# A decoder layer on one core: the first modulation shared out anew between TensorE and VectorE, an S5 exponential on GpSimd, other chunk and load orders

## The chip, the cores and the metric

One core of a Trainium2 chip runs the whole program. The metric is the device time of one execution in microseconds (us); what the kernel before is judged by is the median of three executions.

## What is computed

One layer (DEPTH is 1) of a hybrid decoder trunk in float32 over 512 tokens of width 1024, batch 1. The parts that matter here:

```python
def _split_in(z): ...        # z = h @ w_in + b_in, cut into u, qk, v, o, i, f, q, k, v, f, gates
dt = jnp.exp(log_dt.astype(f32))[:, None]        # first S5 exponential
mag = jnp.exp(dt * are)                          # second S5 exponential
ang = dt * aim
abar_r, abar_i = mag * jnp.cos(ang), mag * jnp.sin(ang)
# _rmsnorm: x * rsqrt(mean(x * x) + EPS) * g
# the layer (adaLN): mod = silu(c) @ mod_w + mod_b, six parts of 1024 columns:
#   h = rmsnorm(x) * norm1_g * (1 + scale) + shift        <- the first two parts
#   x = x + gate * mixer(h);  the second half of the layer, SwiGLU, uses the other parts
```

The mixer sends h through one projection `w_in` (5134 columns), runs three token mixers on it (S5 state space, mLSTM, forgetting attention), merges them by gates and projects by `w_out`; a SwiGLU FFN of width 2816 follows. The first modulation, its 2048 columns `shift` and `scale`, stands ahead of everything: without it there is no h and no projection.

## The kernel before, in words

The program is written engine by engine; each engine runs its list in order and waits on semaphores. Activations lie transposed: `h` is 8 blocks (`KB`) of 128 channels by 512 tokens. Each float32 factor is split in a high and a low part, and a product of 128 by 128 weights with a block of h is three matmuls of 512 columns (lines 1623 to 1625: h_lo by whi, h_hi by whi, h_hi by wlo).

**Chunks.** `w_in` is used in 42 chunks of up to 128 columns, in the order of `A_CHUNKS`: first chunk f (the 14 gate columns, spread over a full tile that GpSimd zeroed before), then u (2), mqk (3), mv (3) and so on. For a chunk s, SP loads `raw`, ScalarE makes the high part (`hi(s)`, line 636), VectorE the low part (`lo(s)`, line 1128), TensorE multiplies (24 matmuls), ScalarE moves the sum out (`evac(s)`). Chunks 0 and 1 are multiplied side by side, block by block of h, because h only then comes into being; from chunk 2 on one follows the other. ScalarE's list around a chunk t is: hi(t), evac(t-3). Chunk s needs lo(s) and evac(s-2). SP's load of chunk s (4 or later) waits until chunk s-4 is multiplied.

**The opening.** SP loads four tiles of x (`xtok`, 0.5 MB each), then eight slabs of `mod_w` (`modA`, `modB`, 1 MB each, 128 rows by 2048 columns) with the small loads of `rows1` behind slab 2 and the three loads of chunk f (line 449, 1024 pieces of 16 or 24 bytes each) behind slab 5. ScalarE's queue loads `rows2` (c, a_re, a_im, log_dt, d). TensorE turns `rows2`, VectorE copies it (`s5c`), ScalarE makes silu(c) (`cf`), squares the tiles of x and takes the root. VectorE meanwhile: exponential of log_dt, 1/root, scaling of the four tiles of x (line 1018, for which TensorE's transposes wait), `vectors()`, the second exponential, the S5 angle scalars (lines 983 to 1040), and then the shift half of the modulation, slab by slab (columns 0 to 1023, lines 987 and 1118). TensorE takes the scale half by `mod_rows(k)`: per slab two matmuls of one weight column and 512 columns (line 1642). The two halves become columns by 8 matmuls each (lines 1667 and 1675) into one bank; VectorE adds the bias (line 1135) and forms the gain (line 1137); only then do ScalarE (lines 734, 735) and VectorE (lines 1147, 1150) make h_hi and h_lo, block by block.

**Behind it** VectorE's list goes lo(2), lo(3), `coefficients()` (S5), four of the eight angle tables, two of the four blocks of B, lo(4), two blocks of B, lo(5), four tables, lo(6) and on.

`keep_clock(n)` is a helper that gives TensorE n matmuls of 256 columns whose result nobody reads; before, it is used at the start of the FFN only.

Of the kernel before, what the change touches and what calls it, by code (L numbers as in the profile page):

```python
# [23 lines left out]
P = 128  # L24
# [31 lines left out]
A_CHUNKS = ([("f", 0)] + [("u", i) for i in range(2)] + [("mqk", i) for i in range(3)]  # L56
# [10 lines left out]

S_UP = NA
# [16 lines left out]
def build(nc, x, c, mod_w, mod_b, norm1_g, norm2_g, w_in, b_in, a_re, a_im, log_dt, b_re, b_im,  # L85
# [3 lines left out]
    with es:  # L89
# [175 lines left out]
        dve_step = sem("dve_step")  # L265
        t_rows = sem("rows_transposed")
# [168 lines left out]
        def _(sp_):  # L437
            for t in range(NT):
                sp_.dma_start(xtok[:, t], x[t * P:(t + 1) * P, :]).then_inc(s_x[t], 16)
            for k in range(KB):  # L440
                sp_.dma_start((modA, modB)[k // 4][:, k % 4], mod_w[k * P:(k + 1) * P, 0:2 * D]
                              ).then_inc(s_mod0[k], 16)
                if k == 2:
                    for src, n, r in ROWS1[5:]:
                        sp_.dma_start(rows1[r:r + n, :], src).then_inc(s_rows1, 16)
                if k == 5:
                    sp_.wait_ge(s_pad, 1)
                    for c0, n, at0 in ((OFF_MF, MH, 0), (OFF_FF, FH, MH), (OFF_MI, MH, 32)):
# [85 lines left out]
        def _(pool):  # L534
            nc.gpsimd.memset(ident[:], 0.0).then_inc(s_const, 1)
# [13 lines left out]
            nc.gpsimd.memset(sst[:, :, :, 0:1], 0.0).then_inc(s_const, 1)  # L549

# [38 lines left out]
        def _(act):  # L589
# [9 lines left out]
            act.dma_start(rows2[96:104, :], row_view(c[0], 8)).then_inc(s_rows, 16)  # L599
# [337 lines left out]
        def _(dve):  # L937
# [1181 lines left out]
```

## Time and profile before

| | us |
|---|---|
| executions | 882.35, 880.01, 877.83 |
| median | 880.01 |
| the profiled execution, its own time | 878.05 |
| its span in the profile | 876.3 |
| TensorE busy | 848.2 (97%) |
| VectorE busy | 440.8 (50%) |
| ScalarE busy | 324.2 (37%) |
| GpSimd busy | 32.9 (4%) |

The span is what the engines' records cover; 1.75 us of the execution lie around it. The median lies 1.96 us above the profiled execution. A timeline row gives start, duration (both us), engine, line and operation, what is written and read with its shape, how often, and in brackets the idle time ahead and what ended it.

### The profile page before, as it was taken

To read this page: it belongs to the slowest core of one execution; us is meant where nothing else is said; L and a number is where in the kernel's file an instruction comes from. 1 tells how busy PE (TensorE), PEld (TensorE's weight loads), DVE (VectorE), ACT (ScalarE), POOL (GpSimd) and SP (SyncE) were. 2 spreads that over 40 slices of the span, in tenths; PEclk is the share of its full clock that TensorE was granted. 3 is DMA by queue.
4 is the path that set the end of the run, shared out by engine and by line. 5 is a ranking of instruction groups with operands and counts; after the bars stand their busy time and mean duration, and the time that the engine had idled before them with its cause. 6 is when DMAs were issued, how large, how long until landed. Compare 5 with 4: busy or idle time off the path is not lost.

```text
span 876.3 us, 10481 instructions
## 1 busy us (share of the span) xinstructions
PE 848.2 (97%) x3914; PEld 678.3 (77%) x3914; DVE 440.8 (50%) x719; ACT 324.2 (37%) x477; POOL 32.9 (4%) x46
## 2 busy tenths in 40 slices
PE   4899999999999999999999999999999999999996
PEld 1477888877878677777888878888888888888886
DVE  4889977246768653334883354333333333322222
ACT  3555444443222543433333544333333332222221
POOL 1010000000000000000001110000000000000110
PEclk9899999999999999999999999999999999999999
DMA  9823422257785112114323324333333333333322
GB/s 366 231 76 88 105 73 73 73 158 253 261 288 169 48 49 65 57 45 148 97 73 121 96 56 114 96 96 96 96 96 96 96 96 90 92 107 90 98 76 96
DMA packets 149372, 100.67 MB, mean 115 GB/s; under 512 B 11072, under 2 KB 142552, under 8 KB 148312
## 3 DMA queue, kind: packets, MB, share of 16 engines
q1 hardware_dynamic: 149096, 100.14, 37.9%
q8 instruction: 22, 0.36, 0.2%
q14 instruction: 14, 0.11, 0.0%
q10 hardware_dynamic: 240, 0.06, 0.0%
HBM read 97.03 MB, written 2.10 MB: 113 GB/s over the span
## 4 chain that ended last, share of the span: by engine, by line
PE 88%; DVE 6%; ACT 3%; issue 1%; DMA 1%; ACTq 0%; DVEq 0%
PE bank L1623 25%; PE bank L1625 25%; PE bank L1624 25%; PE bank L1832 2%; PE bank L1762 1%; PE bank L1854 1%; PE bank L1782 1%; PE bank L1793 1%; PE bank L1642 1%; DVE wlo L1128 1%; PE bank L1879 1%; PE bank L1845 1%; PE bank L1830 1%; DMA rows<-in_s_d 1%; ACT whi L636 1%
## 5 line engine op out<-in xcount | busy, mean ns | idle before, releaser
L1623 PE MATMUL bank<-h_lo,whi 128*128 128x512 f32 x712 | 286.7, 403 | 4.0 <-DVE h_lo L1150 2.2
L1625 PE MATMUL bank<-h_hi,wlo 128*128 128x512 f32 x712 | 279.3, 392 | 0.0
L1624 PE MATMUL bank<-h_hi,whi 128*128 128x512 f32 x712 | 278.8, 392 | 0.0
L1623 PEld LDWEIGHTS bank<-h_lo,whi 128*128 128x128 f32 x712 | 134.9, 189 | 34.8 <-issue 5.9
L1624 PEld LDWEIGHTS bank<-h_hi,whi 128*128 128x128 f32 x712 | 135.0, 190 | 28.8 <-issue 1.7
L1625 PEld LDWEIGHTS bank<-h_hi,wlo 128*128 128x128 f32 x712 | 134.5, 189 | 29.0
L1128 DVE TENSOR_TENSOR wlo<-raw,whi 128x1024 fp32r<-128x1024 f32 x61 | 74.4, 1223 | 104.3 <-ACT whi L636 104.3
L636 ACT ACTIVATE whi<-raw 128x1024 fp32r<-128x1024 f32 x61 | 64.2, 1055 | 153.2 <-PE bank L1625 110.1
L1625 PE MATMUL bank<-a_hi,wlo 128*128 128x512 f32 x176 | 68.5, 389 | 0.0
L1623 PE MATMUL bank<-a_lo,whi 128*128 128x512 f32 x176 | 68.5, 389 | 0.0
L1624 PE MATMUL bank<-a_hi,whi 128*128 128x512 f32 x176 | 68.5, 389 | 0.0
L1585 DVE TENSOR_TENSOR wlo<-raw,whi 128x1024 fp32r<-128x1024 f32 (+1 forms) x24 | 27.3, 1137 | 76.3 <-ACT whi L904 76.3
L1566 DVE TENSOR_TENSOR aa<-sil,bank 128x512 f32<-128x512 f32 x22 | 15.1, 687 | 99.0 <-PE bank L1625 99.0
L1578 DVE TENSOR_TENSOR wlo<-raw,whi 128x1024 fp32r<-128x1024 f32 x40 | 49.0, 1225 | 28.3 <-ACT whi L897 27.0
L897 ACT ACTIVATE whi<-raw 128x1024 fp32r<-128x1024 f32 x40 | 42.1, 1053 | 30.2 <-DMA raw<-in_ffn_w 30.2
L904 ACT ACTIVATE whi<-raw 128x1024 fp32r<-128x1024 f32 (+1 forms) x24 | 23.7, 988 | 67.9 <-DMA raw<-in_ffn_w 67.9
L888 ACT ACTIVATE a_hi<-aa 128x512 f32 x20 | 12.6, 632 | 96.8 <-DVE aa L1566 96.8
L1384 DVE SCALAR_TENSOR_TENSOR macc<-slab,cf,macc 128x1024 f32<-128x1024 f32 x28 | 36.0, 1287 | 6.5 <-DMA slab<-in_mod_w 4.6
L709 ACT ACTIVATE pf<-bank,nmx 128x128 f32<-128x128 f32 (+3 forms) x24 | 12.6, 527 | 69.6 <-PE bank L1845 48.9
L1624 PEld LDWEIGHTS bank<-a_hi,whi 128*128 128x128 f32 x176 | 33.0, 188 | 6.9
L1625 PEld LDWEIGHTS bank<-a_hi,wlo 128*128 128x128 f32 x176 | 33.0, 188 | 6.9
L1623 PEld LDWEIGHTS bank<-a_lo,whi 128*128 128x128 f32 x176 | 33.0, 188 | 6.8
(325 smaller groups left out, 983.5 us busy)
## 6 DMA issues: line engine op xcount, KB each, us to landing
raw<-in_ffn_w SPq DMA_DIRECT2D x60, 512.0 KB, 3.8
raw<-in_w_in SPq DMA_DIRECT2D x44, 512.0 KB, 4.0
slab<-in_mod_w SPq DMA_DIRECT2D x32, 512.0 KB, 6.0
modA<-in_mod_w SPq DMA_DIRECT2D x4, 1024.0 KB, 12.1
modB<-in_mod_w SPq DMA_DIRECT2D x4, 1024.0 KB, 11.1
raw<-in_w_out SPq DMA_DIRECT2D x8, 512.0 KB, 3.7
raw<-in_ffn_w SPq DMA_DIRECT2D x8, 384.0 KB, 3.3
xtok<-in_x SPq DMA_DIRECT2D x4, 512.0 KB, 5.2
```

Of the source, the lines that this page charges most:

```text
L636: A(w_high(s), raw[:, s % 4], ACT.Copy).then_inc(w_hi, 1)
L897: A(whi4[:, s % 4], raw[:, s % 4], ACT.Copy).then_inc(w_hi, 1)
L904: A(whi4[:, s % 4, 0:nk], raw[:, s % 4, 0:nk], ACT.Copy).then_inc(w_hi, 1)
L1128: V.tensor_tensor(wlo[:, s % 4], raw[:, s % 4], w_high(s).bitcast(F32), ALU.subtract).then_inc(w_lo, 1)
L1384: ins = V.scalar_tensor_tensor(out=macc[g][:], in0=slab[:, q % 4], scalar=cf[:, k:k + 1], in1=macc[g][:], op0=ALU.mult, op1=ALU.add)
L1566: V.tensor_tensor(aa[:, u], sil[:, u], ps[2 * u + 1][:], ALU.mult).then_inc(s_act, 1)
L1578: V.tensor_tensor(wlo[:, s % 4], raw[:, s % 4], whi4[:, s % 4].bitcast(F32), ALU.subtract).then_inc(w_lo, 1)
L1585: V.tensor_tensor(wlo[:, s % 4, 0:nk], raw[:, s % 4, 0:nk], whi4[:, s % 4, 0:nk].bitcast(F32), ALU.subtract).then_inc(w_lo, 1)
L1623: mm(dst, w_h, m_l, start=first, stop=False)
L1624: mm(dst, w_h, m_h, start=False, stop=False)
L1625: return mm(dst, w_l, m_h, start=False, stop=last)
L1832: mm(b, qpad[:, h, t * P:(t + 1) * P], kf[:, h // 2, 0:ln], start=False, stop=True).then_inc(s_fs, 1)
```

## The change

Six things:

- **Chunk order.** f stands behind the three mqk chunks, as chunk 5 (`S_F`). Its three loads are issued in the loop, once chunk 1 is multiplied, and not between the slabs. hi and lo of it handle 14 columns in two instructions each, not 128. The fill of its tile on GpSimd is gone.
- **Loads.** c and a_re go through SP, between the first and the second tile of x (ScalarE's queue keeps a_im, log_dt, d). The loads of `rows1` come behind slab 1. The loads of chunks 0, 1, 2 come right behind slab 7. The 16 moves of u come at s = 8, not 9.
- **Second exponential on GpSimd**, `decay()`: 30 instructions of 128x8 in a chain (VectorE has fused forms, GpSimd takes two instructions for those), from T3 = dt * a_re, which VectorE now makes as soon as dt is there. `coefficients()` waits for its end (`s_mag`).
- **First modulation.** VectorE sums columns 0 to 1279 into `macc1st`, TensorE 1280 to 2047 (512 and 256 wide). On VectorE the angle scalars and slab 0 come ahead of the scaling of x, slabs 1 to 7 behind it, `vectors()` behind slab 2; slab 7 is taken in three pieces.
- **h in two halves.** The columns for blocks 0 to 3 (shift and scale) go to bank 7, those for 4 to 7 to bank 6; bias and gain are formed half by half (`mod_halves`). ScalarE and VectorE begin blocks 0 to 3 with the first half; lo(1) stands between the low parts of blocks 0 and 1.
- **Fill matmuls.** `keep_clock(7)` ahead of the slabs, `keep_clock(2, 3)` ahead of chunk 0.

VectorE's list from the end of the first exponential to lo(1). Before (`sp` are the S5 scalars, `modA` and `modB` the slabs, `gs_55` the gain):

```order
L990 SCALAR_TENSOR_TENSOR sp<-sp,spi 128x8 [waits dve_step]
L1016 RECIPROCAL rstd<-rstd 128x4 [waits std_ready,dve_step]
L1018 TENSOR_SCALAR xtok<-xtok,rstd 128x1024 [waits dve_step]
L1018 TENSOR_SCALAR xtok<-xtok,rstd 128x1024 x3
L965 COPY vec<-bank 128x128 [waits rows_transposed]
L983 TENSOR_TENSOR sp<-sp,s5c 128x8
L1040 TENSOR_SCALAR sp<-sp 128x8 [waits dve_step]
L987 TENSOR_SCALAR modA<-modA,cf 128x1024 [waits mod_first_loaded0,silu_c_ready,dve_step]
L1118 SCALAR_TENSOR_TENSOR modA<-modA,cf 128x1024 [waits mod_first_loaded1,dve_step]
L1128 TENSOR_TENSOR wlo<-raw,whi 128x1024 [waits w_hi_ready] x2
L1135 TENSOR_TENSOR modc<-bank,vec 128x16 [waits mod_first_columns]
```

and now:

```order
L1071 TENSOR_TENSOR sp<-sp,s5c 128x8
L1088 TENSOR_SCALAR sp<-sp 128x8 [waits dve_step]
L1172 TENSOR_SCALAR macc1st<-modA,cf 128x1280 [waits mod_first_loaded0,silu_c_ready,s5_scalar_inputs]
L1163 RECIPROCAL rstd<-rstd 128x4 [waits std_ready,dve_step]
L1165 TENSOR_SCALAR xtok<-xtok,rstd 128x1024 x3
L1174 SCALAR_TENSOR_TENSOR macc1st<-modA,cf,macc1st 128x1280 [waits mod_first_loaded1]
L1174 SCALAR_TENSOR_TENSOR macc1st<-modB,cf,macc1st 128x512 [waits mod_first_loaded7,dve_step]
L1174 SCALAR_TENSOR_TENSOR macc1st<-modB,cf,macc1st 128x256
L1190 TENSOR_TENSOR wlo<-raw,whi 128x1024 [waits w_hi_ready]
L1198 TENSOR_TENSOR modc<-bank,vec 128x2x4 [waits mod_first_columns]
L1223 TENSOR_TENSOR h_lo<-hs,h_hi 128x512 [waits h_hi_ready,dve_step]
L1190 TENSOR_TENSOR wlo<-raw,whi 128x1024 [waits w_hi_ready]
```

The angle scalars and slab 0 moved ahead of the scaling of x, the second exponential left, and only lo(0) now stands ahead of the first bias and gain.

SP's queue from the slabs to the loop over chunks. Before:

```order
L441 DMA modA<-in_mod_w 128x2048 x3
L445 DMA rows_136<-in_b_in 24x128
L441 DMA modB<-in_mod_w 128x2048 x2
L449 DMA raw<-in_w_in 128x8x4 [waits padding_zeroed]
L449 DMA raw<-in_w_in 128x8x6
L449 DMA raw<-in_w_in 128x8x4
L441 DMA modB<-in_mod_w 128x2048 x2
L451 DMA raw<-in_w_in 128x8x128
L452 DMA bsrc<-in_s_b_re 128x8x16
```

and now:

```order
L453 DMA modA<-in_mod_w 128x2048 x2
L457 DMA rows_138<-in_b_in 24x128
L453 DMA modB<-in_mod_w 128x2048 x4
L459 DMA raw<-in_w_in 128x8x128 x3
L460 DMA bsrc<-in_s_b_re 128x8x16
L484 DMA raw<-in_w_in 128x8x128 [waits w_chunk_multiplied]
L480 DMA raw<-in_w_in 128x8x4 [waits w_chunk_multiplied]
L480 DMA raw<-in_w_in 128x8x6
L480 DMA raw<-in_w_in 128x8x4
L484 DMA raw<-in_w_in 128x8x128 [waits w_chunk_multiplied] x3
```

The piecewise loads of f left the place ahead of slabs 6 and 7 and stand between the loads of chunks 4 and 6.

TensorE's list between the last slab and chunk 0. Before, and below it now:

```order
L1667 MATMUL bank<-ones,modrow 128x1 [waits mod_row_copied]
L1667 MATMUL bank<-ones,modrow 128x1 x3
L1675 MATMUL bank<-ones,modA 128x1 [waits mod_first_summed_dve]
L1675 MATMUL bank<-ones,modA 128x1 x7
L1623 MATMUL bank<-h_lo,whi 128x512 [waits h_lo_ready,w_lo_ready]
```

```order
L1737 MATMUL bank<-ones,macc1st 128x1 [waits mod_first_summed_dve,columns_copied]
L1737 MATMUL bank<-ones,macc1st 128x1 x3
L1737 MATMUL bank<-ones,macc1st 128x1 [waits mod_first_summed_dve]
L1743 MATMUL bank<-ones,modrow 128x1 [waits mod_row_copied]
L1743 MATMUL bank<-ones,modrow 128x1 x3
L1731 MATMUL bank<-ones,ident 128x256 x2
L1696 MATMUL bank<-h_lo,whi 128x512 [waits w_lo_ready,h_lo_ready]
```

The sixteen column matmuls stay sixteen, in two groups of eight, and two fill matmuls follow.

The diff, cut:

```diff
-A_CHUNKS = ([("f", 0)] + [("u", i) for i in range(2)] + [("mqk", i) for i in range(3)]
+A_CHUNKS = ([("u", i) for i in range(2)] + [("mqk", i) for i in range(3)] + [("f", 0)]
...
+        DVE_COLS = 1280
+        PE_COLS = ((1280, 1792), (1792, 2048))
...
-            for t in range(NT):
+            sp_.dma_start(xtok[:, 0], x[0:P, :]).then_inc(s_x[0], 16)
+            sp_.wait_ge(s_zero, 1)
+            sp_.dma_start(rows2[96:104, :], row_view(c[0], 8)).then_inc(s_rows, 16)
+            sp_.dma_start(rows2[0:8, :], a_re.rearrange("(i g) n -> i (g n)", g=2)).then_inc(s_rows, 16)
+            for t in range(1, NT):
...
-                if k == 5:
-                    sp_.wait_ge(s_pad, 1)
-                    for c0, n, at0 in ((OFF_MF, MH, 0), (OFF_FF, FH, MH), (OFF_MI, MH, 32)):
-                        sp_.dma_start(raw[:, 0, :, at0:at0 + n],
...
+                if s == S_F:
+                    for c0, n, at0 in ((OFF_MF, MH, 0), (OFF_FF, FH, MH), (OFF_MI, MH, 32)):
+                        sp_.dma_start(raw[:, s % 4, :, at0:at0 + n],
...
-                if s == 9:
+                if s == 8:
                     sp_.wait_ge(s_evac, A_CHUNKS.index(("u", 1)) + 1)
...
+            pool.wait_ge(s_t3, 1)
+            decay()
...
-                A(w_high(s), raw[:, s % 4], ACT.Copy).then_inc(w_hi, 1)
+                if s == S_F:
+                    A(w_high(s)[:, :, 0:10], raw[:, s % 4, :, 0:10], ACT.Copy)
+                    A(w_high(s)[:, :, 32:36], raw[:, s % 4, :, 32:36], ACT.Copy).then_inc(w_hi, 1)
...
-            act.wait_ge(s_modc, 2)
             for k in range(KB):
+                act.wait_ge(s_modc, 2 + 2 * (k // 4))
...
             def coefficients():
 
                 dve.wait_ge(s_trig, 2)
+                dve.wait_ge(s_mag, 1)
...
+            for k in range(KB):
+                if k == 1:
+                    dve.wait_ge(s_std, 1)
+                    link(V.reciprocal(rstd[:], rstd[:]))
...
+                if k == 3:
+                    vectors()
                 dve.wait_ge(s_mod0[k], 16)
...
             lo(0)
-            lo(1)
...
+            mod_halves(0)
             dve.wait_ge(s_xnc, KB)
             for k in range(KB):
+                if k == 1:
+                    lo(1)
+                if k == 2:
+                    mod_halves(1)
...
+            keep_clock(7)
             for k in range(KB):
                 mod_rows(k)
...
+            mod_row_columns(7, 0, range(10, 12)).then_inc(s_mod1, 1)
+            mod_row_columns(6, 0, range(12, 14))
+            pe.wait_ge(s_modd, 3)
+            mod_columns(6, range(4, 8))
+            pe.wait_ge(s_mrowc, 2)
+            mod_row_columns(6, 1, range(14, 16)).then_inc(s_mod1, 1)
+            keep_clock(2, 3)
```

## Rows read from the trace of the kernel before

**Rows 1.** The page, part 2: granted TensorE clock in 40 slices of 21.9 us

```profile
PEclk9899999999999999999999999999999999999999
```

**Rows 2.** Timeline of TensorE: opening, chunks 0 to 4, fill matmuls of the FFN

```profile
12.24 5.82 PE L1642 MATMUL bank<-modA,cf 128*1 128x512 f32 x8 [2.94 <-DMA modA<-in_mod_w]
...
18.75 1.09 PE L1653 MATMUL bank<-ident,xtok 128*128 128x128 f32 x8 [0.43 <-DVE xtok L1018]
19.78 1.88 PE L1642 MATMUL bank<-modA,cf 128*1 128x512 f32 x4
...
34.75 1.94 PE L1667 MATMUL bank<-ones,modrow 1*128 1x1 f32 x16
36.62 3.04 PE L1675 MATMUL bank<-ones,modA 128*128 128x1 f32 x16
41.86 0.77 PE L1623 MATMUL bank<-h_lo,whi 128*128 128x512 f32 x1 [2.20 <-DVE h_lo L1150]
...
55.85 0.47 PE L1623 MATMUL bank<-h_lo,whi 128*128 128x512 f32 x1 [0.19 <-ACT fz L645]
...
67.98 0.50 PE L1623 MATMUL bank<-h_lo,whi 128*128 128x512 f32 x1 [0.96 <-DVE wlo L1128]
...
502.11 1.89 PE L1659 MATMUL bank<-ones,ident 128*128 128x256 f32 x8
```

**Rows 3.** Timeline of VectorE, from the scaling of x to lo(4)

```profile
15.74 0.18 DVE L1016 RECIPROCAL rstd<-rstd 128x4 f32<-128x4 f32 x1 [2.67 <-ACT rstd L618]
15.96 2.74 DVE L1018 TENSOR_SCALAR xtok<-xtok,rstd 128x1024 f32<-128x1024 f32 x4
18.61 0.28 DVE L965 COPY vec<-bank 128x128 f32<-128x128 f32 x1
...
23.28 0.17 DVE L983 TENSOR_TENSOR sp<-sp,s5c 128x8 f32<-128x8 f32 x1
...
26.53 0.75 DVE L987 TENSOR_SCALAR modA<-modA,cf 128x1024 f32<-128x1024 f32 x1
27.32 3.92 DVE L1118 SCALAR_TENSOR_TENSOR modA<-modA,cf 128x1024 f32<-128x1024 f32 x3
...
39.70 0.17 DVE L1135 TENSOR_TENSOR modc<-bank,vec 128x16 f32<-128x16 f32 x1 [0.90 <-PE bank L1675]
...
49.49 0.69 DVE L1150 TENSOR_TENSOR h_lo<-hs,h_hi 128x512 fp32r<-128x512 f32 x1 [0.47 <-ACT h_hi L735]
...
66.71 1.22 DVE L1128 TENSOR_TENSOR wlo<-raw,whi 128x1024 fp32r<-128x1024 f32 x1
```

**Rows 4.** Timeline of ScalarE

```profile
34.86 0.59 ACT L718 ACTIVATE modrow<-bank 1x512 f32<-1x512 f32 x1 [0.27 <-PE bank L1642]
35.35 1.99 ACT L636 ACTIVATE whi<-raw 128x1024 fp32r<-128x1024 f32 x2
40.11 0.81 ACT L735 ACTIVATE h_hi<-xnT,modc,gs 128x512 fp32r<-128x512 f32 x1 [2.77 <-DVE gs L1137]
```

**Rows 5.** Timeline of the DMA queues: when each issue began, how long it held its queue

```profile
2.75 0.41 ACTq L603 DMA_DIRECT2D rows<-in_s_d  x1
...
7.94 16.39 SPq L449 DMA_DIRECT2D raw<-in_w_in  x3
...
25.95 2.90 SPq L452 DMA_DIRECT2D bsrc<-in_s_b_re  x1
```

**Rows 6.** Line 449 (the three loads of f) and line 441 (the slabs): time from issue to landing

```profile
DMA to landing us min/median/max: 6.4/16.5/17.2
...
DMA to landing us min/median/max: 5.2/12.1/17.3
```

**Rows 7.** Windows of 1 us: length, each engine's busy time, granted clock, DMA share, GB/s

```profile
37.00:38.00 1.00, 1.00 (x8) 1.00 (x8) 1.00 (x2) 0.34 (x1) 0.00 (x0) 0.62 0.64 128
47.00:48.00 1.00, 1.00 (x5) 0.75 (x5) 0.86 (x2) 0.87 (x3) 0.00 (x0) 0.76 0.00 0
```

**Rows 8.** GpSimd groups by shape: busy and mean ns of one | idle before

```profile
L585 POOL TENSOR_TENSOR sqa<-sqa,sq 128x512 f32<-128x512 f32 x5 | 6.4, 1285 | 63.3 <-ACT sq L910 63.3
```

More of the change, by code:

```diff
@@ L401, in build @@
         for s in range(S_F1):
-            count[s % 4] += 16 * (3 if s == 0 or S_UP <= s < S_OUT else 1)
+            count[s % 4] += 16 * (3 if s == S_F or S_UP <= s < S_OUT else 1)
             SLOT_LOADS[s] = count[s % 4]
@@ L598, in _ @@
             act.wait_ge(s_zero, 1)
-            act.dma_start(rows2[96:104, :], row_view(c[0], 8)).then_inc(s_rows, 16)
-            act.dma_start(rows2[0:8, :], a_re.rearrange("(i g) n -> i (g n)", g=2)).then_inc(s_rows, 16)
             act.dma_start(rows2[32:40, :], a_im.rearrange("(i g) n -> i (g n)", g=2)).then_inc(s_rows, 16)
@@ L1008, in exact_exp @@
                 stt(o, c_(POL), 1.0, two_k, ALU.add, ALU.mult)
-                if om1 is not None:
-                    tt(om1, c_(POL), two_k, ALU.mult)
-                    stt(om1, two_k, -1.0, om1, ALU.add, ALU.add)
-            exact_exp(c_(DT), None, ldt)
-            dve.wait_ge(s_std, 1)
-            link(V.reciprocal(rstd[:], rstd[:]))
-            for t in range(NT):
-                V.tensor_scalar(xtok[:, t], xtok[:, t], rstd[:, t:t + 1], None, ALU.mult).then_inc(s_xn, 1)
-            vectors()
-            tt(c_(T3), c_(DT), are, ALU.mult)
-            exact_exp(c_(MAG), c_(EM1), c_(T3))
+            exact_exp(c_(DT), ldt)
+            V.tensor_tensor(c_(T3), c_(DT), are, ALU.mult).then_inc(s_t3, 1)
             tt(c_(ANG), c_(DT), aim, ALU.mult)
@@ new lines, in mod_halves @@
+            def mod_halves(half):
+                k0 = 4 * half
+                dve.wait_ge(s_mod1, half + 1)
+                pair = modc[:, 0:16].rearrange("p (v k) -> p v k", k=KB)[:, :, k0:k0 + 4]
+                V.tensor_tensor(pair, ps[7 - half][:, 0:16].rearrange("p (v k) -> p v k", k=KB)[:, :, k0:k0 + 4],
+                                vec[:, V_MOD:V_MOD + 16].rearrange("p (v k) -> p v k", k=KB)[:, :, k0:k0 + 4],
+                                ALU.add).then_inc(s_modc, 1)
+                dve.wait_ge(s_modc, 2 * half + 1)
+                V.scalar_tensor_tensor(out=gs1[:, k0:k0 + 4], in0=modc[:, 8 + k0:12 + k0], scalar=1.0,
+                                       in1=vec[:, V_N1 + k0:V_N1 + k0 + 4], op0=ALU.add, op1=ALU.mult
+                                       ).then_inc(s_modc, 1)
+                dve.wait_ge(s_modc, 2 * half + 2)
@@ L1640, in mod_rows @@
                 pe.wait_ge(s_mod0[k], 16)
[L1641 to L1643 removed]
+                for n, (c0, c1) in enumerate(PE_COLS):
+                    ins = mm(ps[4 + n][0:1, 0:c1 - c0], cf[:, k:k + 1], (modA, modB)[k // 4][:, k % 4, c0:c1],
                              start=(k == 0), stop=(k == KB - 1))
```

155 lines of the change are left out of this document (100 added, 55 removed).

## The prediction

> **What bounds the kernel now.** First the busy shares and the clock row of the page: TensorE is busy 97% of the span at full clock except near the start [rows 1]. Then TensorE's timeline, for its gaps: of its 28 us of idle time the long gaps lie before 68 us, and the 808 us behind it are the same work after the change. So the change is worth what it takes from one moment, the start of chunk 4 at 67.98 [rows 2]. Everything else is read backwards from there.
>
> At 67.98 TensorE had waited 0.96 us for VectorE's lo(4), which ended at 67.93; the last h_lo ended at 50.18 [rows 3]. VectorE works those 17.75 us without a break, on lo(2), lo(3) and S5, none of which the change shortens. TensorE needs for its own part: chunk 0 from 41.86, chunks 2 and 3 from 55.85, 11.2 us, ready at 67.0. So two chains end together there, VectorE's last, TensorE's 1 us ahead. Both start with h_hi of block 0 at 40.11 [rows 4], and that with the last columns of the modulation.
>
> Before it: the SP queue is held 16.39 us by the three loads of f, and slabs 6 and 7 are issued only at 24.4 [rows 5]. Slab 0 landed at 12.2, slab 5, issued at about 7.4 with the longest way, 17.3, at 24.7: 2.5 us per slab [rows 6]. They were not what was late: VectorE came to slab 0 only at 26.53, behind scaling, second exponential and angle scalars, and had all at 36.5.
>
> **The change part by part.** All on the clock of the profiled execution (span 876.3, its own time 878.05).
>
> *rows2.* ScalarE's queue issues d at 2.75; two issues ahead of it (0.6 and 0.3 us) go to SP. Gain between 0 (if only the shared engines count) and 0.9 us; I take 0.65, since the way from issue to landing, 5.7 us, is far longer than an issue and needn't shrink. VectorE ended its first exponential at 13.07 (15.74 less 2.67), now 12.4.
>
> *VectorE up to slab 7.* Angle scalars 23.28 to 26.1 [rows 3], with T3 2.9 us: 15.3. Slab 0 on 1280 columns 0.95 (0.75 for 1024): 16.3. Reciprocal 0.2, scaling 2.74: x is scaled at 19.25, against 18.7 before, 0.55 later. Slabs 1 to 6: 3.92 / 3 = 1.31 for 1024 columns, 1.62 for 1280, so 6 times 1.62 = 9.7, with vectors() 0.6: 29.6. Slab 7 lands at 24.7 + 2 * 2.5 = 29.7, the same moment; its three pieces (0.7, 0.3, 0.6) are done at 30.4, 30.7 and 31.3. Before: 36.5. Most of this is order and the exponential (3.85 us from 19.2 to 23.1), not the split, which costs VectorE 7 * 0.31 + 0.2 = 2.4 us.
>
> *TensorE.* From 18.75 to 34.75 it did four pairs of transposes (1.03 us each), six slabs and 1.1 us of waiting [rows 2], so 1.8 us per slab; with 768 columns of 1024, 1.36. The 1.1 us went with ScalarE, which stood in its list at the sines behind the angle scalars; these come early now. From 19.4: 4.1 + 8.2, rows done at 31.7. Eight columns of the first group take 2.3 us (half of 1.94 + 3.04, less for the full clock): 34.1.
>
> *ScalarE and lo(0).* Two row copies (0.59 and, on 256 columns, 0.35 [rows 4]) end at 32.3; hi(0) 1.0: 33.35; lo(0) 1.22: 34.6. It stands ahead of the bias, so it decides, not the columns at 34.1. Bias and gain 0.4 (39.70 to 40.11): h_hi(0) starts at 35.05, against 40.11: 5.05 us earlier. Half of h stands first, but this half costs lo(1) and a second bias between blocks: hs(3) on ScalarE waits for h_lo(1), 0.4 us later than before. Last h_lo at 35.05 + 10.07 + 0.4 = 45.6, against 50.18. VectorE's chain then gives lo(4) at 45.6 + 17.75 = 63.35.
>
> *TensorE's chain.* The second group of eight columns at half clock ends at 36.6. The fill of two: eight records are 1.89 at full clock [rows 2], so 4 are 0.95, or 1.8 at half: start of chunk 0 at 38.3. Before, the clock fell to half at 37.4 and came back at 47.4 [rows 7], 2.6 us into the sixteen column matmuls. The same sixteen stand there now, so I let it fall at 34.4 and return at 44.4. Then 14 matmuls at 0.427 and 34 at 0.228: chunk 1 done at 52.1. With 11.2 for chunks 2 and 3 and 0.3 for the evacuation: 63.6. Chunk 4 starts at the later of the two chains, 63.65: **4.3 us earlier.** If the clock doesn't fall, TensorE is ready at 59 and VectorE's 63.35 decides: 4.6.
>
> *The f loads.* Issued when chunk 1 is done, 52.2. Their landing is needed by hi(5), ahead of evac(2) in ScalarE's list, and chunk 4 needs evac(2): 0.26 + 0.67, so by 62.5. Nearest rows: bsrc, also 1024 pieces, held SP 2.9 us; the last of the three f loads landed 6.4 after its issue. 0.4 + 2.9 + 6.4 = 9.7: 61.9, hidden by 0.6 us. The other end is 18.3 (7.94 to 19.85 + 6.4), then with shared queues. I take the first, for here no slabs stand ahead.
>
> *GpSimd.* 30 instructions of 128x8 from 12.5 on. Bounds: 0.17 us as on VectorE, 1.29 as for 128x512 [rows 8]; by columns it is nearer to the small one. 6 to 40 us, done between 19 and 52. coefficients() starts at 45.6 + 2.3 = 47.9, so anything under 1.1 us per instruction is hidden.
>
> *Nothing each:* f behind mqk (lo(5) is 0.9 us shorter, but stands behind the start of chunk 4), the moves of u (needed at chunk 8), keep_clock(7): 3 us at full clock, 6 at half, from 8.2, over before VectorE has scaled x at 19.25 even with slabs 0 and 1 behind it.
>
> **The rivals.**
>
> *1. TensorE goes cold in new gaps.* Between turning rows1 at 17 and the first x at 19.4 it now stands 2.4 us, and with full clock 4 us ahead of chunk 4. At 12.24 two slabs took 5.82 where 3.6 is the full-clock price, though the window's clock reads 1.00: after idling it began at half and lost 2.2 us. Paid once, the gain is 2.1. For it: that row. Against: it stood at the very start of TensorE's work, and the gap of 0.43 us at 18.75 cost nothing. The Trainium skill, TensorE: Matmul & The Clock Gate, section HAM oscillation — how this bites in real kernels, says that waits between bursts of matmuls bring the clock back to half and that each burst then begins cold; of a 2.4 us gap no run here shows whether it is enough.
>
> *2. Slower: f lands late.* If the three loads need 18.3 us as before, they land at 70.5, evac(2) ends at 71.5 and chunk 4 starts at 71.6, 3.6 us later than before. It loses from 14.7 us of loading on. For it: SP's 16.39. Against: a ring full of slabs stood ahead of them then. The Trainium skill, DMA: Bandwidth & Descriptors, section Why small descriptors are slow (HBM only), says that each descriptor carries fixed costs; the row agrees that the size in bytes says nothing, 56 KB in all.
>
> *3. The start is elsewhere late.* rows2 no earlier, slab 7 later by 1 to 2 us because c, a_re and three chunks share the queue, or GpSimd near its upper bound: gain 0 to 1.
>
> *4. More than summed.* Slabs land faster without f among them and rows2 gains all of 0.9; the clock holds: 5.5 to 7.
>
> **How the numbers follow.** The sum, gain 3 to 5.3: 0.54. Rival 1: 0.20. Rival 2: 0.07. Rival 3: 0.09. Rival 4: 0.10. The forecast is the sum: 880.0 - 4.3 = 875.7; the profiled span would be 872.0. Its own range is 874.7 to 877.0. The range for 8 in 10 takes in rivals 1 and 3 and most of 4, and the 2 us by which single executions lie about their median: 871.5 to 880.5. Rival 2 is left out. About 0.5%, 4.4 us, is what a measurement of this kernel can tell from no change, and the sum stands right at it: faster gets 0.54 * 0.5 + 0.10 = 0.37, slower the worse half of rival 2 and a rest, 0.07, the same what is left, 0.56.
>
> **What would show it.** In the timeline of after: x scaled at about 19.3; slab 7 taken from 29.7 on; h_hi(0) at 35 behind lo(0); the last h_lo at 45.6; lo(4) at 63.3 and chunk 4 at 63.7. GpSimd's chain over before 48. The wait ahead of chunk 4 names lo(4) or evac(2): the second is rival 2. Windows of the clock at 19 to 23 and 34 to 45 tell rival 1. I am wrong if any work behind chunk 4 waits anew, or if ScalarE or the DMA queues and not VectorE set h_hi(0).

## The result, and the profile after

The changed kernel takes **872.79 us** (median of 12 executions; one of them, at 1072.1 us, was disturbed and is left out of the ratio, the other 11 lie from 871.62 to 878.64 with a median of 872.29), against 881.01 us (12 executions, 875.36 to 882.76) for the kernel before, measured beside it. The ratio is 0.9926, with a 95% interval of 0.9907 to 0.9946: 0.74% faster. The forecast was 875.7 us, the range 871.5 to 880.5. The profiled execution of after took 872.08 us, its span is 870.3 (forecast 872.0); before it was 878.05 and 876.3.

The clock row of the page of after is that of [rows 1], digit for digit: 40 slices are too coarse for what changed. The busy shares of the page:

```profile
PE 847.0 (97%) x3932; PEld 681.4 (78%) x3932; DVE 438.8 (50%) x703; ACT 323.8 (37%) x478; POOL 48.2 (6%) x75
```

TensorE's timeline of after, answering to [rows 2] (start, busy time, engine, line, operation, count, and in brackets the idle time before it with what ended it):

```profile
17.86 1.09 PE L1725 MATMUL bank<-ident,xtok 128*128 128x128 f32 x8 [1.15 <-DVE xtok L1165]
18.88 1.45 PE L1715 MATMUL bank<-modA,cf 128*1 128x512 f32 x4
...
30.66 1.45 PE L1715 MATMUL bank<-modB,cf 128*1 128x512 f32 x4 [1.15 <-DMA modB<-in_mod_w]
32.04 1.50 PE L1737 MATMUL bank<-ones,macc1st 128*128 128x1 f32 x12
33.47 1.05 PE L1743 MATMUL bank<-ones,modrow 1*128 1x1 f32 x8
...
51.38 0.47 PE L1696 MATMUL bank<-h_lo,whi 128*128 128x512 f32 x1 [0.19 <-ACT uj L710]
...
63.49 0.50 PE L1696 MATMUL bank<-h_lo,whi 128*128 128x512 f32 x1 [0.95 <-DVE wlo L1190]
```

Chunk 4 starts at 63.49, against 67.98: 4.49 us earlier, behind the same wait for VectorE's lo(4). Chunks 2 and 3 begin at 51.38, against 55.85. TensorE's rows are done at 32.0 instead of 34.75, behind a slab 7 that was waited for. VectorE, answering to [rows 3]:

```profile
6.34 0.22 DVE L1019 COPY rows<-ldt 8x128 f32<-8x128 f32 x1 [4.58 <-DMA rows<-in_s_d]
...
11.05 0.16 DVE L1042 TENSOR_TENSOR sp<-sp,s5c 128x8 f32<-128x8 f32 x1
...
13.93 0.89 DVE L1172 TENSOR_SCALAR macc1st<-modA,cf 128x1280 f32<-128x1280 f32 x1
...
15.06 2.74 DVE L1165 TENSOR_SCALAR xtok<-xtok,rstd 128x1024 f32<-128x1024 f32 x4
...
30.61 1.81 DVE L1174 SCALAR_TENSOR_TENSOR macc1st<-modB,cf,macc1st 128x512 f32<-128x512 f32 x3 [1.05 <-DMA modB<-in_mod_w]
33.54 1.23 DVE L1190 TENSOR_TENSOR wlo<-raw,whi 128x1024 fp32r<-128x1024 f32 x1 [1.11 <-ACT whi L696]
34.69 0.16 DVE L1198 TENSOR_TENSOR modc<-bank,vec 128x8 f32<-128x8 f32 x1
...
44.99 0.69 DVE L1223 TENSOR_TENSOR h_lo<-hs,h_hi 128x512 fp32r<-128x512 f32 x1 [0.53 <-ACT h_hi L796]
...
62.22 1.22 DVE L1190 TENSOR_TENSOR wlo<-raw,whi 128x1024 fp32r<-128x1024 f32 x1
```

The first modulation is summed at 32.4 instead of 36.5, the last h_lo ends at 45.68 instead of 50.18, and from there to the end of lo(4) at 63.44 it is 17.76 us, as before (17.75). ScalarE, answering to [rows 4]: the copies of the rows, then hi(0) and hi(1), then h_hi(0), at 35.11 instead of 40.11.

```profile
31.71 0.85 ACT L779 ACTIVATE modrow<-bank 1x512 f32<-1x512 f32 x2 [4.86 <-PE bank L1715]
32.47 1.04 ACT L696 ACTIVATE whi<-raw 128x1024 fp32r<-128x1024 f32 x1
34.15 1.06 ACT L696 ACTIVATE whi<-raw 128x1024 fp32r<-128x1024 f32 x1 [0.64 <-DMA raw<-in_w_in]
35.11 0.80 ACT L796 ACTIVATE h_hi<-xnT,modc,gs 128x512 fp32r<-128x512 f32 x1
```

**From 4.5 us to 6.0 in the span, and 8.2 in the medians.** From 73.6 to 235 us an instruction of after stands 4.5 us ahead of the same one of before; from 242 us on it is 6.1, and 5.9 at the end (the matmul at 866.18 before is at 860.25). What lies between is a stretch of the profiled kernel before at the lower clock of 1.2 GHz, right behind the sixteen one-column matmuls of a later modulation. First the timeline of before, then its windows (length, busy time and count of each engine, granted clock, DMA share, GB/s):

```profile
233.05 1.84 PE L1879 MATMUL bank<-ones,macc 128*128 128x1 f32 x16
234.75 0.48 PE L1623 MATMUL bank<-h_lo,whi 128*128 128x512 f32 x1
...
236.23 0.63 PE L1624 MATMUL bank<-h_hi,whi 128*128 128x512 f32 x1
...
238.96 0.39 PE L1625 MATMUL bank<-h_hi,wlo 128*128 128x512 f32 x1
```

```profile
235.00:236.00 1.00, 1.00 (x4) 0.75 (x4) 1.00 (x2) 0.00 (x0) 0.00 (x0) 0.61 0.89 328
236.00:237.00 1.00, 1.00 (x4) 0.80 (x3) 0.90 (x5) 0.00 (x0) 0.00 (x0) 0.50 0.42 160
237.00:238.00 1.00, 1.00 (x4) 0.72 (x3) 1.00 (x3) 0.01 (x1) 0.00 (x0) 0.50 0.10 41
238.00:239.00 1.00, 1.00 (x5) 0.82 (x4) 1.00 (x3) 1.00 (x3) 0.00 (x0) 0.69 0.00 0
```

TensorE is busy throughout, but a matmul takes 0.63 us there and not 0.39. The clock is at half for 3.4 us, half of which is lost, 1.7 us; the instructions behind it show 1.6. After has the same sixteen matmuls (at 228.57) and keeps a clock of 1.00 behind them. These stretches come and go from execution to execution, and, as the runs below show, more in some kernels than in others.

### The profile page after: what moved, and what is told of

Same layout as the page of the kernel before. It is cut to its first block, busy times and chain, and to the rows that moved or that the text cites. A ratio compares the mean times of both kernels' runs of the same rounds, so it can differ in the third digit from the quotient of the medians.

```text
span 870.3 us, 10546 instructions
## 1 busy us (share of the span) xinstructions
PE 847.0 (97%) x3932; PEld 681.4 (78%) x3932; DVE 438.8 (50%) x703; ACT 323.8 (37%) x478; POOL 48.2 (6%) x75
## 4 chain that ended last, share of the span: by engine, by line
PE 87%; DVE 5%; DMA 3%; ACT 2%; issue 1%; SPq 1%; DVEq 0%; ACTq 0%
PE bank L1696 25%; PE bank L1698 25%; PE bank L1697 25%; DMA raw<-in_w_in 3%; PE bank L1913 2%; PE bank L1843 1%; PE bank L1935 1%; PE bank L1863 1%; PE bank L1874 1%; DVE wlo L1190 1%; PE bank L1960 1%; ACT whi L696 1%; PE bank L1926 1%; PE bank L1911 1%; PE bank L1815 0%
```

## The experiments

Two quantities are read from each profile: the **start of chunk 4**, and the half-clock time behind it. In all 14 profiles the span is the start of chunk 4, plus 806.8 us, plus 0.5 us for each microsecond of half clock behind it, within 0.5 us. Half clock comes in pieces of about 3.4 us (1.7 us lost). So a term of the sum can be read as a shift of chunk 4, and the luck of the late stretches stays apart. The last column counts the executions whose granted clock averaged at least 0.993 over the span (at most three such pieces in all), and gives the median of these alone. The pieces ahead of chunk 4 count too, and the profiles have one to three of them there (before three, after two): so the column sorts executions roughly, and it is not a count of late stretches.

```
kernel                         chunk 4   lost behind it   span    median (n)    ratio [95%]             clock >= 0.993
before                         67.98     1.7              876.3   881.01 (12)   -                       19 of 79, 876.2 to 876.7 *
after                          63.49     0                870.3   872.79 (12)   0.9926 [0.9907,0.9946]  9 of 11, 872.25
after, run again               64.07     1.7              872.5   873.88 (4)    0.9923 [0.9897,0.9949]  3 of 4, 873.51
exponential on VectorE         68.43     1.7 **           877.2   878.95 (10)   0.9982 [0.9962,1.0002]  2 of 10, 876.2
no fills                       64.51     5.1              876.2   877.41 (10)   0.9957 [0.9938,0.9976]  1 of 10, 874.32
lo(4) first                    61.6 ***  1.7              869.6   873.14 (6)    0.9934 [0.9901,0.9967]  4 of 6, 871.73
f alone on before              67.55     6.8              881.0   880.64 (10)   0.9995 [0.9967,1.0023]  4 of 10, 876.04
after without fills of 7       63.44     3.4              873.2   873.63 (4)    0.9917 [0.9890,0.9943]  3 of 4, 873.41
after without fills of 2       63.29     5.1              874.7   874.45 (10)   0.9937 [0.9919,0.9955]  4 of 10, 873.34
before with fills of 7         67.02     5.1              878.6   878.83 (10)   0.9985 [0.9958,1.0012]  4 of 10, 875.93
before with fills of 2         67.65     6.8              880.8   880.67 (12)   1.0003 [0.9978,1.0027]  2 of 12, 877.05
split 1024/1024                64.07     5.1              875.5   873.98 (10)   0.9942 [0.9915,0.9970]  7 of 10, 873.36
exponential on GpSimd alone    66.66     0                873.6   879.74 (10)   0.9991 [0.9968,1.0015]  2 of 10, 875.96
h begun once                   65.65     5.1              877.3   879.97 (10)   1.0007 [0.9979,1.0034]  1 of 10, 873.35
*   the runs of before beside the three groups of experiments; medians by group
**  three more pieces of half clock lie ahead of chunk 4, at 20 to 28 and 41 to 45
*** no wait stands there; worked out from the transposes behind it, below
```

Two runs of the changed kernel itself differ by 0.58 us in the start of chunk 4 (63.49 and 64.07), so a shift below about 0.7 us says nothing there by itself. The source of this scatter can be read from the traces: VectorE takes up slab 7, when it has landed, at 30.61 in after, and at 31.20, 31.66, 30.57 and 30.42 in after run again, without fills, without fills of 7 and without fills of 2; chunk 4 starts 32.85 to 32.88 us behind that in all five. Counted from this moment a shift of 0.1 us can be told.

On the kernel before the scatter is larger, about 1 us: with fill matmuls, which should move nothing, chunk 4 stands at 67.02 and 67.65 and not at 67.98. VectorE's bias can wait there for the sixteen column matmuls (0.90 us in before), and their second half (line 1675) takes 3.04 us in before, where the clock falls early in it, 2.58 with the fills of 2 and 1.95 with the fills of 7.

**The second exponential back on VectorE.** My theory (A in the expectations) was the sum of the prediction, part by part, with the exponential as its largest part.

```diff
-            V.tensor_tensor(c_(T3), c_(DT), are, ALU.mult).then_inc(s_t3, 1)
+            tt(c_(T3), c_(DT), are, ALU.mult)
+            exact_exp(c_(MAG), c_(T3))
...
-            pool.wait_ge(s_t3, 1)
-            decay()
```

> The changed kernel with one part undone: the second S5 exponential (19 instructions of 128x8 with the two squarings) is on VectorE again, between the first exponential and the angle scalars. Theory A (x and the rows of TensorE set the first h): VectorE scales x 4.2 us later, 19.3 instead of 15.1; TensorE's transposes and slabs take 12.4 us behind it, so its rows end at 34.6, not 32.1; h_hi(0) and the start of chunk 4 move by 2.4 us, to 65.9, and the time is 2.4 us above the changed kernel's. Theory B (the landing of slab 7 sets it): VectorE waited 2.9 us for slabs 5 to 7 in the changed kernel, which take up most of the exponential; chunk 4 moves by 0.5 us or less.

Chunk 4 went back to 68.43, 4.94 us later than in after: the whole gain and a little more. The chain is the one expected, its size is not: 2.4 us were expected. VectorE begins the angle scalars at 15.62 instead of 11.05, and x is scaled 4.5 us later (4.2 expected). TensorE's timeline shows what is added to that:

```profile
22.39 1.97 PE L1727 MATMUL bank<-ident,xtok 128*128 128x128 f32 x8 [5.53 <-DVE xtok L1167]
24.29 2.72 PE L1717 MATMUL bank<-modA,cf 128*1 128x512 f32 x4
26.93 1.35 PE L1727 MATMUL bank<-ident,xtok 128*128 128x128 f32 x8
28.21 1.45 PE L1717 MATMUL bank<-modA,cf 128*1 128x512 f32 x4
...
68.43 0.80 PE L1698 MATMUL bank<-h_lo,whi 128*128 128x512 f32 x1 [2.52 <-DVE wlo L1192]
```

```profile
22.00:24.00 2.00, 1.61 (x8) 1.57 (x8) 1.96 (x3) 0.46 (x1) 0.00 (x0) 0.50 1.00 418
24.00:26.00 2.00, 2.00 (x5) 0.26 (x4) 1.93 (x6) 0.73 (x2) 0.00 (x0) 0.50 1.02 426
26.00:28.00 2.00, 2.00 (x10) 1.14 (x9) 1.97 (x4) 0.12 (x1) 0.00 (x0) 0.62 0.99 414
```

After a gap of 5.53 us the clock reads 0.50: the transposes take 1.97 us instead of 1.09 and the slab 2.72 instead of 1.45, 2.15 us more. That is the mechanism of rival 1, at its price. In after the gap at this place is 1.15 us and the clock stays at 1.00. The exponential on GpSimd therefore saves its own time on VectorE, and also keeps TensorE from a long gap. The ratio of 0.9982 says the same: without this part little is left of the gain.

**No fill matmuls.** Both `keep_clock` calls are out of the changed kernel.

> The changed kernel without its nine fill matmuls. Theory A (VectorE's chain sets chunk 4): chunk 0 starts at 37.9 behind lo(1) and not at 38.2; the half-clock stretch may be longer, up to the 10 us of the kernel before, which makes TensorE ready for chunk 4 at 63.9 at worst against lo(4) at 63.4: chunk 4 within 0.5 us of 63.5, time within 0.5 us. Theory B (the fills are what keeps the clock): slabs 0 and 1 run at half, the stretch begins before the column matmuls and chunk 4 starts 1.5 us or more later.

Chunk 4 starts at 64.51. All of the 1.0 us comes from the DMA queues: slab 7 was taken up 1.05 us later (31.66, after 30.61), and from there to chunk 4 it is 32.85 us, as in after (32.88). x was scaled later too, at 18.7 instead of 17.8, but that is not what sets chunk 4: in the run without the fills of 2 it was scaled 0.5 us later than in after, and chunk 4 started 0.2 us earlier. The median was 4.6 us above that of after, with two late stretches in the profile (at 299 and 368 us):

```profile
367.00:368.00 1.00, 1.00 (x4) 0.62 (x3) 0.00 (x0) 0.78 (x3) 0.00 (x0) 0.79 0.48 143
368.00:370.00 2.00, 2.00 (x3) 0.28 (x1) 0.00 (x0) 1.91 (x4) 0.00 (x0) 0.50 0.00 0
...
372.00:374.00 2.00, 2.00 (x8) 1.70 (x7) 1.11 (x2) 0.00 (x0) 0.00 (x0) 0.50 0.00 0
```

Theory B was right in one point that cost nothing: without the fills slabs 0 and 1 took 4.15 us together (5.26 in the run below without the seven), against 1.45 each behind them; TensorE waits for the scaling of x behind these slabs, and that wait takes it up.

So a second theory was formed: fills near the start keep the clock hundreds of microseconds later. The four runs with single fills, below, were made for it.

**lo(4) first.** If VectorE's list is what holds chunk 4, then moving two of its B blocks behind lo(4) frees it.

```diff
-                if t == 3:
+                if t == 4:
                     b_block(3)
                     b_block(2)
-                if t == 4:
                     b_block(1)
```

> The changed kernel with VectorE's first two blocks of B moved from ahead of lo(4) to behind it. Theory A (TensorE's 0.95 us ahead of chunk 4 is VectorE's S5 work, and there is slack behind): lo(4) ends at 59.5, chunk 4 starts at 62.5 as chunk 3 ends, 0.95 us earlier, and stays that much earlier: lo(5) ends at 67.7 as now and chunk 5 then needs it at 68.1. Time 0.9 us below the changed kernel's. Theory B (the wait only moves): the 0.95 us come back ahead of chunk 5 or 6 and the time stays.

The wait ahead of chunk 4 is gone; TensorE runs through to the transposes of c within chunk 4 at 67.14, against 69.07 in after:

```profile
66.92 0.39 PE L1697 MATMUL bank<-h_hi,wlo 128*128 128x512 f32 x1
67.14 0.60 PE L1780 MATMUL bank<-ident,cdup 128*128 128x128 f32 x4
```

That is 1.93 us less, of which 0.95 is the wait and 0.7 an earlier start of chunk 2 (50.70; slab 7 was taken up 0.66 us earlier, at 29.95); 0.3 is left over. It shows that VectorE's S5 work, not TensorE, set the start of chunk 4, and that nothing behind took the gain back in the profiled execution (span 869.6; its fastest execution, 869.62 us, is the lowest of all). The median, 873.14 us, is not below that of after; among executions with few stretches it is 871.73 against 872.25. It is not shown to be faster.

**f alone.** The kernel before with f as chunk 5, its loads behind chunk 1, and chunks 0 to 2 loaded right behind slab 7.

> The kernel before with one part alone: chunk f behind the mqk chunks, its loads in the loop, two small instructions each for its parts, chunks 0 to 2 loaded behind slab 7. Theory A (VectorE's list sets the opening, the slabs are not late for it): slabs 6 and 7 are issued by 9 us and not at 24.4, but VectorE still comes to slab 0 at 26.5; chunk 4 stays at 68.0 within 0.3 us and the time is that of before. Theory B (the pieces of f slowed the opening): chunk 4 is 1 us or more earlier. In both the clock stretch behind 34 us is that of before, since the sixteen column matmuls and no fill stand there.

Chunk 4 at 67.55 against 67.98, a little outside the 0.3 us that were expected and within the scatter of this kernel; ratio 0.9995: nothing, as the sum had it. The slabs landing earlier don't help a VectorE that comes to them late.

**The changed kernel again, and the fills one by one.** Four kernels: after unchanged; after without `keep_clock(7)`; after without `keep_clock(2, 3)`; before with `keep_clock(7)` ahead of its slabs.

> The changed kernel once more, as the mate of the next three on the same chip. Account: every profile so far is chunk 4's start plus 806.8 us plus 1.7 us for each 3.4 us at half clock behind it. Chunk 4 at 63.5 within 0.7 us, as often as not no stretch behind it: median 872 to 873.5. If the many executions at mean clock 0.995 were chance, the median is above 875.

> The changed kernel without the seven fill matmuls ahead of the slabs, with the two ahead of chunk 0. Theory A (the early seven are what keeps most executions free of late half-clock stretches): mean clock 0.988 in most executions and a median of 876 to 878, as without both fills. Theory B (the late two do it, or nothing does): clock 0.995 in most and a median of 872 to 874.

> The changed kernel with the seven fill matmuls and without the two ahead of chunk 0. Chunk 0 starts at 37.9 or so behind lo(1), chunk 4 stays at 63.5 within 0.7 us since VectorE sets it. Theory A: mean clock 0.995 in most executions, median 872 to 873.5. Theory B (the two do it): 0.988 in most, median 876 to 878.

> The kernel before with seven fill matmuls ahead of the slabs and nothing else. They lie beside the wait for slab 0 and the scaling of x, so chunk 4 stays at 68.0 within 0.5 us. Theory A: late stretches become rare, mean clock 0.99 or more in most executions, median about 877 instead of 880.6. Theory B: clocks 0.986 to 0.988 in half of them as before and a median of 880 to 881.

Chunk 4 stands at 64.07, 63.44 and 63.29, and at 67.02 against 67.98: no fill moves it beyond the scatter. The medians are 873.88, 873.63, 874.45 and 878.83. Without the seven fills nothing is lost (873.63 beside 873.88, on one chip), and put into before they leave 0.9985, an interval that holds 1. Nothing here supports the theory that the seven keep the clock. Without the two ahead of chunk 0, 4 of 10 executions were well clocked, against 12 of 15 of after in its two runs: this pointed at the two.

**The kernel before with two fills ahead of chunk 0.**

```diff
             mod_shift_columns()
+            pe.wait_ge(s_xnc, KB)
+            keep_clock(2, 3)
```

> The kernel before with the two fill matmuls ahead of chunk 0 and nothing else. They take 1.8 us at half clock in the 2.2 us that TensorE waits there, so chunk 4 stays at 68.0 within 0.5 us. Theory A (the two are what makes late half-clock stretches rare: so far 19 of 25 executions with them had a mean clock of 0.993 or more, 5 of 20 without them in the changed kernel's family): 0.993 or more in two of three executions, median 877. Theory B (the split of the executions is chance, or comes with the rest of the change): 0.986 to 0.989 in more than half, median 880 to 881.

Ratio 1.0003, 2 of 12 executions well clocked (before: 11 of 35 beside it). The two fills alone don't keep the clock either.

**The split back to 1024 columns each** (`DVE_COLS = 1024`, the column matmuls four and four).

> The changed kernel with the first modulation split 1024 to 1024, so with h still in two halves. Theory A (the landing of slab 7 at 30.6 sets both engines, as their waits ahead of slabs 5 to 7 say): VectorE is done with slab 7 0.3 us earlier, TensorE's last slab takes 1.85 instead of 1.4 us, and its rows end 0.45 us later, which lo(0) covers in part: chunk 4 later by 0.5 us at most. Theory B (TensorE's 3.6 us less of slab work were on the path): 1.5 us or more.

Chunk 4 at 64.07, 0.58 us later than the profiled after. Slab 7 was taken up at 30.61 in both, so this is the split and not scatter. The 1280 columns give TensorE time that it mostly doesn't need while both engines wait for the slabs; what counts is the last slab, 1.88 us instead of 1.45, and ScalarE's second row copy, 0.59 instead of about 0.3: worth 0.6 us.

**The exponential on GpSimd alone**, on the kernel before.

```diff
+            pool.wait_ge(s_t3, 1)
+            decay()
...
-            exact_exp(c_(MAG), c_(T3))
...
+                dve.wait_ge(s_mag, 1)
```

> The kernel before with the second exponential on GpSimd and nothing else moved. VectorE's list up to the last slab is 4.2 us shorter: slab 7 done at 32.3, if it has landed by 31, not at 36.5. Theory A (then TensorE is the next bound, its rows end at 33.9 since ScalarE's sines come 4 us earlier, and sixteen columns take 5 us): bias at 38.7, chunk 4 at 67.0, 1.0 us earlier than before. Theory B (the exponential is the whole gain): 3.5 to 4.5 us earlier.

```profile
32.60 1.88 PE L1689 MATMUL bank<-modB,cf 128*1 128x512 f32 x4 [0.66 <-DMA modB<-in_mod_w]
34.41 1.94 PE L1714 MATMUL bank<-ones,modrow 1*128 1x1 f32 x16
36.28 1.95 PE L1722 MATMUL bank<-ones,modA 128*128 128x1 f32 x16
40.52 0.76 PE L1670 MATMUL bank<-h_lo,whi 128*128 128x512 f32 x1 [2.29 <-DVE h_lo L1197]
```

Chunk 4 starts at 66.66, 1.3 us earlier than in before, where taking the same part out of after cost 4.9. Even of the 1.3 us a part may be luck of the clock: the column matmuls of line 1722 took 1.95 us here, as in before with the fills of 7, whose chunk 4 is at 67.02; beside that run the gain is 0.4 us. TensorE, behind a slab 7 that lands at 32.6 (f's loads still stand ahead of it) and with all 32 narrow matmuls ahead of h, is the next bound. The parts don't add: the exponential frees VectorE, and the order of loads, TensorE's shorter rows and the halves of h must be there for this to arrive at chunk 4.

**h begun once.** The changed kernel, with both halves of bias and gain formed before block 0.

```diff
-                act.wait_ge(s_modc, 2 + 2 * (k // 4))
+                act.wait_ge(s_modc, 4)
...
             mod_halves(0)
+            mod_halves(1)
...
-                if k == 2:
-                    mod_halves(1)
```

> The changed kernel with h begun once, when all sixteen columns are there; order of the columns and fills unchanged. The second group of columns ends at 36.7 in the changed kernel, 2.2 us behind the first. Theory A: h_hi(0) starts at 37.1 instead of 35.1; the 0.4 us of the second bias between the blocks goes ahead of them; last h_lo 1.6 to 2.0 us later, chunk 4 at 65.3. Theory B (TensorE's chain at half clock is the bound): chunk 4 within 0.5 us of 63.5.

ScalarE now waits 1.40 us for the gain, and chunk 4 starts at 65.65:

```profile
37.25 0.81 ACT L796 ACTIVATE h_hi<-xnT,modc,gs 128x512 fp32r<-128x512 f32 x1 [1.40 <-DVE gs L1202]
...
65.65 0.50 PE L1695 MATMUL bank<-h_lo,whi 128*128 128x512 f32 x1 [1.59 <-DVE wlo L1190]
```

h_hi(0) is at 37.25 instead of 35.11, and chunk 4 2.16 us later. The copies of the rows, ahead of all that was changed, already stood 0.72 us later (32.43, after 31.71), for slab 7 was taken up at 31.33 and not at 30.61; from there to chunk 4 it is 34.32 us, where after has 32.88. The halves of h are therefore worth 1.4 us, the length of the wait. This is the second part that carries the gain, and a larger one than the split that came with it. With both calls of `keep_clock` in it, only 1 of 10 executions was well clocked (median 879.97).

## Why the prediction was right, and where not

**The bound and the place.** Right: the gain is decided at chunk 4, behind lo(4), in two chains that end within a microsecond of each other in the profiled execution. Forecast 63.65, measured 63.49, and a gain of 4.49 where the sum had 4.3. Taking VectorE's blocks away (lo(4) first) took the wait away.

**rows2.** Too small. The copy that waits for them stands at 6.34, and before at 8.49: 2.15 us earlier where I took 0.65 and set 0.9 as the upper end. d was issued 0.7 us earlier (2.04, before 2.75), and its way got shorter by 1.4 us. That the way "needn't shrink" was the step that failed. It is no chance of one run: TensorE turns these rows at 6.03 to 7.65 in the nine profiles of the changed kernel and its variants, and at 8.85 to 8.94 in the five of before and its own. Why the way got shorter is open, for no run moves these loads alone. x was scaled at 17.8 (forecast 19.25).

**Slabs.** Too early in the forecast. I let slab 7 land at 29.7 and bind no one. It came at 30.6, and slabs 5 and 6 were waited for as well (0.91 and 0.89 us), so VectorE was done at 32.4 (forecast 31.3). The two errors have opposite signs and nearly cancel: x came 1.4 us too early, and the wait for slabs ate it. That h_hi(0) then stood where the sum had it is luck: in after's second run slab 7 landed 0.6 us later, and chunk 4 started 0.6 us later. It also meets a sign that the prediction had named for being wrong, "if ScalarE or the DMA queues and not VectorE set h_hi(0)": both TensorE (1.15 us) and VectorE (1.05) waited for slab 7, and VectorE then waited 1.11 us for ScalarE's hi(0) ahead of lo(0). Behind the change it is the landing of slab 7 that sets chunk 4, as the five profiles with 32.85 to 32.88 us between the two show; less work for either engine ahead of slab 7 gains nothing more. The windows of after show the queues at work all this time: the DMA share is full, first at 419 and then at 294 GB/s.

```profile
20.00:28.00 8.00, 7.54 (x38) 3.32 (x36) 6.11 (x9) 3.26 (x6) 7.08 (x12) 1.00 1.01 419
28.00:34.00 6.00, 4.79 (x25) 2.51 (x25) 3.82 (x5) 1.80 (x3) 1.74 (x3) 1.00 1.15 294
```

**TensorE's rows, ScalarE, lo(0).** Rows done at 32.0 (forecast 31.7), VectorE's last piece 1.1 us later than forecast, but the chain from TensorE's rows over ScalarE was the one that decided, as the part on lo(0) had it: hi(0) ends at 33.5, lo(0) runs to 34.77 (34.6), h_hi(0) stands at 35.11 (35.05). Second half: `hs(3)` waited 0.51 us (forecast 0.4). Last h_lo 45.68 (45.6); lo(4) ends at 63.44 (63.35). The run with h begun once took this term out and lost 1.4 us beside slab 7.

**TensorE's clock.** Half clock from 35.0 to 41.9, where I let it be 34.4 to 44.4 as before. Its chain was ready at 62.5 instead of 63.6, and the measured wait of 0.95 us for lo(4) is this difference. It had no weight, since VectorE decided. Of rival 1: the gap ahead of the first x was 1.15 us, not 2.4, and cost nothing. But in after's second run rival 1 came true ahead of chunk 4: half clock in the opening lasted 3.4 us and not 6.8, so TensorE came earlier, waited 2.51 us for lo(4) and lost 1.7 us behind it. From chunk 4 at 64.07 the gain of 3.9 us comes down to 2.2, close to the 2.1 that rival 1 had. Its row, the 5.82 us of slabs 0 and 1 at a clock that "reads 1.00", holds no contradiction: the trace's record of the clock begins only at 16.76 us in before (11.14 in after), and ahead of that the windows read 1.00 whatever the matmuls take.

**The f loads.** Rival 2 is far off: three loads of 1024 pieces held SP for 2.95 us together, the last landed 4.0 us after its issue, at 56.6, and hi(5) took them at 57.20, where it had waited for TensorE and not for them. I had taken 9.7 us for the whole, and 18.3 as the other end.

**GpSimd.** The 30 instructions ran from 11.22 to 29.90, 0.62 us each with the gaps, within the bounds and 18 us ahead of their use at 48.15. "By columns nearer to the small one" holds only while VectorE is not in a long operation (below).

**The rest of the program.** "The 808 us behind it are the same work" is true of the work and not of its time. In the profiled pair this gives 1.5 us that no term had; in the medians the difference is 8.2 us where 4.5 are explained. Among well clocked executions before stands at 876.2 to 876.7 and after at 872.25 and 873.51: 2.7 to 4.5 us, which fits the part from chunk 4. The remaining 3.7 us of the medians go with the clock: 60 of 79 executions of before are below 0.993, against 3 of 15 of after, and the median clocks are 0.988 and 0.995. One kind is understood, the one behind a long wait for chunk 4 (last section). What makes those further on rarer in after is **open**: not the seven fills, not the two fills alone, and the changed kernel with h begun once has both and still shows them. One rival is untested: that it is the moment at which the later narrow matmuls come, and so the shift itself, that counts. The six rows of the table whose chunk 4 starts by 64.1 have 30 of 45 executions at 0.993 or more, the other eight 35 of 151; but the six also share most of the change. I had also put "within 0.5%" ahead of "faster"; with 0.74% measured it was the less likely case that came, and it came through these stretches.

## What to carry to other kernels

Find the one moment from which the rest runs without waiting, and price every edit as a shift of that moment; read what moved there, not the median alone. Parts of such a change don't add up: the same exponential was worth at most 1.3 us alone and 4.9 us within the whole, since each part only uncovers the next bound, and a gap that grows from 1.2 to 5.5 us also costs TensorE its clock. When TensorE is 97% busy, look at its granted clock behind the stretches of narrow matmuls before ascribing a difference of medians to an edit.

## What the runs showed of the hardware

**The clock behind the wait for chunk 4.** Four profiles have a wait of 1.91 us or more there (1.91, 2.18, 2.51, 2.52), and in all four the clock fell to half within 1.5 us behind it, for 1.7 us lost; the row and the windows of after's second run show it:

```profile
64.07 0.50 PE L1696 MATMUL bank<-h_lo,whi 128*128 128x512 f32 x1 [2.51 <-DVE wlo L1190]
```

```profile
62.00:64.00 2.00, 0.00 (x0) 0.00 (x0) 1.97 (x4) 1.29 (x2) 0.00 (x0) 1.00 0.62 137
64.00:66.00 2.00, 1.93 (x5) 1.55 (x6) 1.93 (x8) 0.00 (x0) 0.00 (x0) 0.62 0.42 125
66.00:68.00 2.00, 2.00 (x6) 1.57 (x5) 1.93 (x8) 0.00 (x0) 0.00 (x0) 0.53 0.00 0
```

The nine with a wait of 0.95 to 1.59 kept it. So rival 1 is real and near: 1 us more of waiting for VectorE costs the 1 us and 1.7 more. The Trainium skill, page TensorE: Matmul & The Clock Gate, section HAM oscillation — how this bites in real kernels, says that waits between bursts bring the clock back to half. These rows agree; the waits of its example are of some 3 to 5 us, where here 1.91 us was enough, and there the measurement decides.

**A busy TensorE loses its clock too.** With no idle time ahead, right behind sixteen one-column matmuls (at 230 to 236 us in three profiles and at 277 in one) or within narrow attention work that follows such matmuls (365 to 373 us, eight profiles), the granted clock fell to 0.50 for 3.4 us or twice that. Waits don't cover these. In five profiles it also fell at 299 to 304 us, within narrow attention work and some 1.5 us behind a wait of 1.0 us for ScalarE; after has the same wait, at 296.65, and kept its clock.

**GpSimd beside VectorE.** One operation on 128x8 took 0.20 to 0.25 us, or up to 1.6 us:

```profile
13.44 0.20 POOL L576 TENSOR_SCALAR sp<-sp 128x8 f32<-128x8 f32 x1
...
19.44 1.47 POOL L573 TENSOR_TENSOR sp<-sp 128x8 f32<-128x8 f32 x1
21.00 0.23 POOL L577 TENSOR_SCALAR sp<-sp 128x8 f32<-128x8 f32 x1
...
23.25 1.47 POOL L573 TENSOR_TENSOR sp<-sp 128x8 f32<-128x8 f32 x1
```

The short ones lie among VectorE's small operations (`vectors()` at 20.89 to 21.5 and the angle scalars). The long ones, 1.4 to 1.6 us, lie under its 1280-column sums, each 1.55 us long (one runs from 23.11 to 24.66): GpSimd got through about when such a sum ended. Under slab 0's multiplication (0.89 us) and the scaling of x (0.7 us each), with one tensor as input, it took 0.55 to 0.87 us. The Trainium skill, page GPSIMD Engine Reference, section Key points, says that its SBUF interfaces are shared with VectorE, with contention when VectorE reads two SBUF inputs, as such a sum does; the trace agrees, and shows that an operation of 0.2 us can wait out nearly a whole instruction of VectorE's.

**Small pieces in a quiet queue.** The same three loads of f held SP 16.39 us behind slabs and 2.95 us once the slabs had landed. The three chunk loads put right behind slab 7 held it for 20.73 us. Most of the time is thus set by what stands ahead; the small pieces of f have a price too, for a single chunk load of 0.5 MB at 50.54 held SP for 0.39 us only.
